# A two-block transformer on one core: the norm stages with column-group sums, small roots and joined phases

## The reference, cut to what matters

```python
def rmsnorm(x, g):
    xf = x.astype(jnp.float32)
    y = xf * lax.rsqrt(jnp.mean(xf * xf, axis=-1, keepdims=True) + RMS_EPS)
    return (y * g.astype(jnp.float32)).astype(x.dtype)
...
x = x + gt1 * rmsnorm_2(y, p['g_post_mix'])
h = modulate(rmsnorm_2(x, p['g_pre_ffn']), sh2, sc2)
x = x + gt2 * rmsnorm_2(conv_ffn(h, p), p['g_post_ffn'])
```

## Time and profile before

| what | us |
|---|---|
| median of 3 runs (lowest to highest) | 3000.8 (2995.47 to 3001.47) |
| the profiled execution | 3002.31 |
| its span, first to last instruction | 3000.5 |
| PE busy (of the span) | 2717.9 (91%) |
| DVE busy | 1418.4 (47%) |
| ACT busy | 516.1 (17%) |
| POOL busy | 162.8 (5%) |
| mean granted TensorE clock | 0.943 |

### The profile page before, as it was taken

One profiled execution on the slowest core, in us unless ns is written; L12 is line 12 of the kernel. 1 busy time (PEld: TensorE's weight loads), 2 busy tenths in 40 slices (PEclk: granted clock), 3 DMA queues, 4 the chain that ended last, 5 costly groups with the idle time before them and its releaser, 6 DMA issues.

```text
span 3000.5 us, 46544 instructions
## 1 busy us (share of the span) xinstructions
PE 2717.9 (91%) x20206; PEld 1974.1 (66%) x20206; DVE 1418.4 (47%) x2486; ACT 516.1 (17%) x1033; POOL 162.8 (5%) x112
## 2 busy tenths in 40 slices
PE   7989999998999898999999988997778769999996
PEld 3643788886645445888884743546777733788885
DVE  3153655525004436555424365254444463877624
ACT  2121100001013322000001032013333211122100
POOL 0000000000000000000000000003333200000000
PEclk9979999999998989999999977997999979999998
DMA  5313222233120002232234101200000013222231
GB/s 189 97 36 98 71 85 85 67 100 100 57 84 1 1 30 83 93 96 84 58 99 128 42 15 56 56 1 2 4 4 4 4 57 98 71 85 84 67 91 53
DMA packets 219563, 190.34 MB, mean 63 GB/s; under 512 B 8667, under 2 KB 216956, under 8 KB 219360
## 3 DMA queue, kind: packets, MB, share of 16 engines
q1 hardware_dynamic: 219066, 187.27, 20.2%
q10 hardware_dynamic: 294, 0.09, 0.0%
HBM read 185.25 MB, written 2.10 MB: 62 GB/s over the span
## 4 chain that ended last, share of the span: by engine, by line
PE 81%; DVE 12%; issue 2%; ACT 2%; DVEq 0%; DMA 0%; POOLq 0%; POOL 0%; ACTq 0%; SPq 0%
PE psum L1138 26%; PE psum L335 18%; PE psum L1348 13%; PE psum L365 4%; PE psum L2041 4%; PE psum L2048 3%; PE psum L778 2%; PE psum L800 2%; DVE sbuf L277 1%; PE psum L786 1%; PE psum L776 1%; DVE sbuf L290 1%; PE psum L2118 1%; PE psum L1751 1%; DVE sbuf L2431 1%
## 5 line engine op out<-in xcount | busy, mean ns | idle before, releaser
L1138 PE MATMUL psum<-sbuf 128*128 128x256 f32 x3696 | 810.6, 383 | 9.9 <-DVE sbuf L1197 6.5
L1138 PEld LDWEIGHTS psum<-sbuf 128*128 128x128 f32 x3696 | 708.7, 192 | 110.8 <-DVE sbuf L1197 7.7
L335 PE MATMUL psum<-sbuf 128*128 128x512 f32 (+5 forms) x1424 | 542.4, 543 | 22.7 <-DVEq L434 22.5
L335 PEld LDWEIGHTS psum<-sbuf 128*128 128x128 f32 (+3 forms) x1424 | 264.5, 187 | 295.8 <-issue 257.1
L1348 PE MATMUL psum<-sbuf 128*128 128x256 f32 x1848 | 405.2, 382 | 12.4 <-DVE sbuf L1365 6.8
L1348 PEld LDWEIGHTS psum<-sbuf 128*128 128x128 f32 x1848 | 353.8, 192 | 63.5 <-DVE sbuf L1365 7.6
L1222 DVE TENSOR_TENSOR sbuf<-sbuf,psum 128x256 f32<-128x256 f32 x462 | 177.7, 415 | 205.7 <-PE psum L1138 204.5
L2048 PE MATMUL psum<-sbuf 64*64 64x64 f32 x4992 | 204.8, 232 | 32.6 <-issue 19.1
L2041 PE MATMUL psum<-sbuf 64*64 64x64 f32 (+1 forms) x4544 | 180.0, 233 | 50.3 <-DVE sbuf L2409 30.6
L2048 PEld LDWEIGHTS psum<-sbuf 64*64 64x64 f32 x4992 | 180.0, 143 | 44.2 <-issue 38.1
L2041 PEld LDWEIGHTS psum<-sbuf 64*64 64x64 f32 x4544 | 164.5, 141 | 57.1 <-DVE sbuf L2409 32.0
(11 more groups left out here) (232 smaller groups left out, 2516.7 us busy)
## 6 DMA issues: line engine op xcount, KB each, us to landing
sbuf<-in_w_mod_dram SPq DMA_DIRECT2D x24, 1024.0 KB, 5.2
sbuf<-in_w_ffn_gate_dram SPq DMA_DIRECT2D x22, 1024.0 KB, 5.5
sbuf<-in_w_ffn_up_dram SPq DMA_DIRECT2D x22, 1024.0 KB, 7.3
sbuf<-in_w_ffn_down_dram SPq DMA_DIRECT2D x32, 704.0 KB, 6.2
...
```

The source lines that it names most:

```text
L335: mm = pe.matmul(bank, w[:, q, c0:c0 + m], rhs(k0 + q), start=start and q == 0, stop=stop and q == kc - 1)
L1138: mm = pe.matmul(bank, w[:, q, :], rhs[:, q, :], start=q == 0, stop=q == 3)
```

## The change

Each norm becomes three small steps. `column_sums` does not make one product of 512 tokens but four of 128, with 32 columns of `k.means` as weights and each with its output in its own 32 partitions of a PSUM bank: the means of the 512 tokens lie in 128 columns and four groups of partitions. ACT takes the root there with epsilon as bias, DVE the reciprocal in place, both over 128x128. `spread_columns` brings them back: four 128x128 products with one column of the identity, broadcast, as weights, into a PSUM bank of 128x512, from which DVE then scales.

In the post-norm the last two squares are no longer added on DVE but summed on PE, the product's phase and the norm phase are one (`joined`), and ACT loads the table with the root at the start of the product's phase (`load_root_table`). In the update POOL adds the chunks 0, 2, 3, 5 and 6 through three buffers in SBUF, DVE the chunks 1, 4 and 7 through one in PSUM. Shifts of the pre-norm go to ACT. The `w_mod` tiles are taken in pairs, with their rows in two groups of 32 partitions and their matmuls in turn; one pair stands before the second norm's first sum, one after its second, and the copy out (two of 2x512) stands on ACT between the squares of chunks 6 and 7. The squares and sums of `aside` in `ffn_up` go one by one behind the units 1 to 8 of the phase.

```diff
...
+def column_sums(k, pe, out, sq, start, stop):
+
+    for t in range(4):
+        r = slice(32 * t, 32 * t + 32)
+        mm = pe.matmul(out[r, :], k.means[:, 0:32], sq[:, t * P:(t + 1) * P], start=start, stop=stop)
+    return mm
+
+
+def spread_columns(k, pe, out, root):
+
+    for t in range(4):
+        mm = pe.matmul(out[:, t * P:(t + 1) * P], k.ident[:, 32 * t:32 * t + 1].broadcast_to([P, P]), root, start=True, stop=True)
+    return mm
...
+POOL_CHUNKS = (0, 2, 3, 5, 6)
+VECTOR_CHUNKS = (1, 4, 7)
+UPDATE_ORDER = (("scale", 0), ("scale", 1), ("scale", 2), ("add", 1), ("scale", 3), ("scale", 4), ("scale", 5), ("add", 4),
+                ("scale", 6), ("scale", 7), ("add", 7))
+TMP_BANK, POST_BANK, PRE_BANK, SUM_BANK = 0, 1, 6, 7
...
+def post_sum_tensor(k, pe, j):
+    pe.wait_ge(j.added, (KD - 3) * (j.nth + 1))
+    column_sums(k, pe, j.sums, j.acc, True, False)
+    for n in (KD - 2, KD - 1):
+        pe.wait_ge(j.squared, KD * j.nth + n + 1)
+        mm = column_sums(k, pe, j.sums, j.sq[:, (n - 1) % 2, :], False, n == KD - 1)
+    mm.then_inc(j.summed, 1)
+
+
+def root_scalar(k, act, j):
+    act.wait_ge(j.summed, j.nth + 1)
+    act.activation(j.root, j.sums, ACT.Sqrt, bias=k.eps).then_inc(j.rooted, 1)
+
+
+def invert_vector(k, dve, j):
+    dve.wait_ge(j.rooted, j.nth + 1)
+    dve.reciprocal(j.root, j.root).then_inc(j.inverted, 1)
...
-def norm_phase(k, name, jobs, post=None):
...
+def norm_phase(k, name, pre, post=None, fills=None):
...
+        if post:
+            spread_tensor(k, pe, post)
+            if not pre:
+                return
+            fill(0)
+            pre_sum_tensor(k, pe, pre, range(0, 2))
+            fill(1)
+            pre_sum_tensor(k, pe, pre, range(2, KD))
+            fill(2)
+            spread_tensor(k, pe, pre)
+        else:
+            pre_sum_tensor(k, pe, pre, range(KD))
+            fill(0)
+            fill(1)
+            spread_tensor(k, pe, pre)
+            fill(2)
...
+        for c in range(KD):
+            pre_square_scalar(k, act, pre, c)
+            if post and fills and fills.scalar and c == KD - 2:
+                fills.scalar(k, act)
...
+                for q in range(KD):
+                    for i in range(2):
+                        mm = pe.matmul(out[own[i], 256 * n:256 * n + 256], self.SIL[:, q, :], w[i][:, q, :],
+                                       start=q == 0, stop=q == KD - 1)
+                        if q == KD - 1:
+                            mm.then_inc(k.half_done, 2)
...
-    post = make_norm(k, "ffn_post2", Y, S, [], A_SCR)
-    ph.append(ffn_down(k, "ffn_down2", 2, k.a["w_down_2"][0], post, "ffn_up2"))
-    ph.append(norm_phase(k, "layer_norm2", [], post=(post, lambda c: derived_col(k, "pf", c))))
+    post = PostNorm(k, Y, lambda c: derived_col(k, "pf", c), A_SCR)
+    stage = ffn_down(k, "ffn_down2", 2, k.a["w_down_2"][0], post, "ffn_up2")
+    ph.append(joined(stage, norm_phase(k, "layer_norm2", None, post)))
```

More of the change, by code:

```diff
@@ new lines, in spread_tensor, with update_vector @@
+def spread_tensor(k, pe, j):
+    pe.wait_ge(j.inverted, j.nth + 1)
+    spread_columns(k, pe, j.rstd, j.root).then_inc(j.spread, 1)
+def update_vector(k, dve, j):
+    own = k.bank[TMP_BANK]
+    dve.wait_ge(j.spread, j.nth + 1)
+    for what, c in UPDATE_ORDER:
+        if what == "scale":
+            if c in POOL_CHUNKS:
+                n = POOL_CHUNKS.index(c)
+                if n >= 3:
+                    dve.wait_ge(j.moved, len(POOL_CHUNKS) * j.nth + n - 2)
+                out = j.tmp[:, n % 3, :]
+            else:
+                n = VECTOR_CHUNKS.index(c)
+                if n >= 1:
+                    dve.wait_ge(j.renewed, 2 * (len(VECTOR_CHUNKS) * j.nth + n))
+                out = own
+            ins = dve.scalar_tensor_tensor(out=out, in0=j.src[:, c, :], scalar=j.gain(c), in1=j.rstd, op0=ALU.mult, op1=ALU.mult)
+            if c in POOL_CHUNKS:
+                ins.then_inc(j.scaled, 1)
+            else:
+                ins.then_inc(j.renewed, 1)
+        else:
+            n = 2 * (len(VECTOR_CHUNKS) * j.nth + VECTOR_CHUNKS.index(c))
+            dve.wait_ge(j.renewed, n + 1)
+            dve.tensor_tensor(k.H[:, c, :], k.H[:, c, :], own, ALU.add).then_inc(j.renewed, 1)
@@ new lines, in update_pool, with wait_updated, __init__ @@
+def update_pool(k, pool, j):
+    for n, c in enumerate(POOL_CHUNKS):
+        pool.wait_ge(j.scaled, len(POOL_CHUNKS) * j.nth + n + 1)
+        pool.tensor_tensor(k.H[:, c, :], k.H[:, c, :], j.tmp[:, n % 3, :], ALU.add).then_inc(j.moved, 1)
+def wait_updated(eng, j, c):
+    if c in POOL_CHUNKS:
+        eng.wait_ge(j.moved, len(POOL_CHUNKS) * j.nth + POOL_CHUNKS.index(c) + 1)
+    else:
+        eng.wait_ge(j.renewed, 2 * (len(VECTOR_CHUNKS) * j.nth + VECTOR_CHUNKS.index(c)) + 2)
+class PreNorm:
+    def __init__(self, k, src, outs, scratch, post=None):
+        self.src, self.outs, self.post = src, outs, post
+        self.sq, self.root = view(k.M, scratch, 2, S), view(k.M, scratch + 2 * S, P)
+        self.sums, self.rstd = k.bank[SUM_BANK][:, P:2 * P], k.bank[PRE_BANK]
+        self.before, k.outs = k.outs, k.outs + KD * len(outs)
+        self.nth, k.pres = k.pres, k.pres + 1
+        self.shifted, k.shifts = k.shifts, k.shifts + (KD if outs[0][2] is not None else 0)
+        self.normed = k.norm_sems["normed"]
+        s = k.pre_sems
+        self.squared, self.consumed, self.summed, self.rooted, self.inverted, self.spread, self.scaled = (s[x] for x in PRE_SIGNALS)
@@ new lines, in scale_vector, with shift_scalar @@
+def scale_vector(k, dve, j):
+    dve.wait_ge(j.spread, j.nth + 1)
+    for gain, dst, shift in j.outs:
+        for c in range(KD):
+            ins = dve.scalar_tensor_tensor(out=dst[:, c, :], in0=j.src[:, c, :], scalar=gain(c), in1=j.rstd,
+                                           op0=ALU.mult, op1=ALU.mult)
+            ins.then_inc(j.normed if shift is None else j.scaled, 1)
+def shift_scalar(k, act, j):
+    for gain, dst, shift in j.outs:
+        if shift is None:
+            continue
+        for c in range(KD):
+            act.wait_ge(j.scaled, j.shifted + c + 1)
+            act.activation(dst[:, c, :], dst[:, c, :], ACT.Identity, bias=shift(c)).then_inc(j.normed, 1)
@@ L511, in scalar @@
     def scalar(k, act):
+        if fills and fills.first_scalar:
+            fills.first_scalar(k, act)
         if post:
[L513 to L516 removed]
+            root_scalar(k, act, post)
+        else:
+            load_root_table(k, act)
+        if not pre:
+            return
+        for c in range(KD):
+            pre_square_scalar(k, act, pre, c)
+            if post and fills and fills.scalar and c == KD - 2:
+                fills.scalar(k, act)
@@ L543, in square_vector @@
[L543 to L558 removed]
+            update_pool(k, pool, post)
@@ L1557, in part @@
         k.plan += 4
-        sync0, vector0, scalar0 = phase.sync, phase.vector, phase.scalar
-        steps = phase.tensor if isinstance(phase.tensor, list) else [phase.tensor]
-        assert len(split) == len(steps)
-        out = k.psum[0:2, 512 * 5:512 * 7]
-        turned = k.bank[5][:, 0:16].rearrange("p (n two) -> p n two", two=2)
+        out = k.bank[5]
+        turned = [k.bank[4 - i][:, 0:8].rearrange("p (n two) -> p n two", two=2) for i in range(2)]
+        own = [slice(32 * i, 32 * i + 2) for i in range(2)]
         def sync(k, sp):
```

351 lines of the change are left out of this document (184 added, 167 removed).

## The result

The changed kernel takes 2927.0 us (median of four runs, 2922.97 to 2930.61) against 3001.1 for the kernel before (2995.47 to 3002.55): ratio 0.9756, 95% interval 0.9738 to 0.9775. The forecast was 2928, in a range of 2915 to 2966. The profiled execution took 2930.61.

What follows compares the result with a forecast made beforehand. PE was busy 91% of the span, with gains where the chain leaves it in norm stages. Terms summed to 73.5 us off 3002.3, giving 2928.8, or 2928 as median; range 2915 to 2945, to 2966 with rivals 2 and 3.

Steps and rivals of the forecast that it cites:

- A: First root of five norm stages: last square to first post-norm scale 4.4 us instead of 8.87 or 7.6; 19.9 saved.
- B: Update and second root, four w_mod stages: first post-norm to first pre-norm scale 14.25 us instead of 19.1; 19.4 saved.
- rival 3: Clock falls to 1.2 GHz at the spreads: D lost, each of four stages gives back about 3; 2945, chance 12%.
- C: Start of the next product: 3.8 us twice (ffn_norm0, ffn_norm1), 3.4 after ffn_norm2, 2.1 after layer_norm1; 13.1 saved.
- D: Clock in ffn_up0 and ffn_up1: without the gap no half-speed stretch behind it; 2.5 us twice, 5.0 saved.
- E: layer_norm0, bound by PE: first pre-norm scale at 740.9 instead of 743.54; 2.6 us saved.
- F: input_norm, bound by PE: pairs from about 31.3 to 40.1, lead at 42.5 instead of 50.16; 7.7 us saved.
- Rivals 1 and 2: 1: column groups take turns, 2982, chance 8%. 2: DVE and POOL still exclude each other, 2939 to 2950, 9%.
- 4 and 5: Rival 4: narrow passes neither overlap nor hold clock, about 3070, 3%. Rival 5: unseen wait holds stages, about 3000, 2%.

Runs made afterwards that it cites:

- late_copies: six_squares with the copies of the w_mod rows behind ACT's second root and their turning behind PE's second spread; 2904.6 us, ratio 0.9684.
- aside_ahead: The changed kernel with the squares and adds of aside back ahead of the first weight sums of ffn_up0 and ffn_up1; 2928.8 us, ratio 0.9762.
- split_pair: late_copies with the second half of the second w_mod pair moved behind the last column sum; 2894.2 us, ratio 0.9666.
- after_again: The changed kernel, unaltered, measured and profiled once more; 2930.2 us, ratio 0.9761.
- serial_tiles: The changed kernel with the w_mod tiles of a pair multiplied one after the other, not in turns; 2939.5 us, ratio 0.9809.
- own_sbuf: The changed kernel with DVE's own product of the update (chunks 1, 4 and 7) in SBUF instead of PSUM; 2930.0 us, ratio 0.9766.
- split_both: split_pair with the second half of layer_norm0's values products also moved behind the last column sum; 2908.6 us, ratio 0.9699.
- six_squares: The changed kernel with six square buffers instead of two in the pre-norm; 2913.8 us, ratio 0.9719.

## Why the prediction held, and where it did not

**A was right in mechanism and 0.6 too long each.** 4.4 was forecast, 3.78 came. The old root of `layer_norm1` was 8.31 and not the 7.6 that I had taken for it, which adds 0.7. The last column sum is 0.43 with its tail where I had 0.7, since the tails of narrow passes overlap, and the spread with its change of weights 1.16 where I had 1.5; the 0.3 in it for changing to full weights had no row behind it, and 1.16 is the 0.86 of the columns and 0.3. The root was 0.37 for 0.27; the row I took was a copy. The three ways of undoing it price its parts: width 2.2, drain 0.25, table 0.8. That is 3.2 of the 5.1 saved in `ffn_norm0`; the rest, the add and the epsilon that left DVE's part of the chain (0.69 each) with their handovers, was not tested by itself.

**B failed, by 8 of 19.** Only the update (7.3 for 7.7) was as forecast. Two steps failed.

The first is the sentence that PE is done at about 9, before ACT. PE's amount of work was right, its order was not looked at: the second pair stands ahead of six sums, and with two square buffers ACT cannot go on without those sums. I had added up each engine's work where the two are coupled chunk by chunk. Where the clock is full, in `layer_norm1` and `ffn_norm2`, this puts the end of the last square at 11.37 instead of 10.25: 1.1 in each of four stages, 4.5.

The second is the clock, which the sum put at nothing in these stages and left to rival 3. These two rows of the changed kernel are the first pair of `layer_norm1` and the second spread of `ffn_norm0`, 30 and 8 passes; the same 30 took 5.09 in `ffn_norm0`, the same 8 take 1.16 in late_copies.

```profile
1546.56 3.40 PE L1760 MATMUL psum<-sbuf 128*2 128x256 f32 x30
```

```profile
283.46 2.08 PE L306 MATMUL psum<-sbuf 128*128 128x128 f32 x8 [1.05 <-DVE sbuf L370]
```

The slow first pair moves the last square to 13.05 and 12.83 in `ffn_norm0` and `ffn_norm1`, 3.1 together; the slow spread costs 0.9 four times; with 0.3 more in the tail that is 7.1. Against these stands that the tail was forecast too long: 4.0, where it is 3.15 with a spread at full clock (`layer_norm0` of aside_ahead, `ffn_norm2` of late_copies). 4.07 came, near the forecast by luck, because half the clock made up for it. 4.5 + 7.1 - 3.4 = 8.2, the 8 that were missing.

So the order is the smaller part of the miss and the clock the larger. They are not independent: with six buffers and later copies, which touch only order and buffers, the second spread is at full clock in all four stages. The distance is then 11.6 to 13.1, below the 14.25 forecast, which had the copies in the chain. Why the first pair is slow in two stages and not in the two others no run shows.

**C and D were right**, at 12.6 for 12.6 in two stages and 11.3 by the way back; the wait of PE went as forecast, and aside_ahead brought both it and the half clock behind it back. After `layer_norm1` the same term failed (-0.6 for 2.1). There the lead, 16 passes at 0.43, ran partly at half clock behind the second root, as these rows of the changed kernel and of split_pair show (in late_copies it takes 7.11):

```profile
1563.75 9.67 PE L507 MATMUL psum<-sbuf 128*128 128x512 f32 x16 [1.69 <-ACT sbuf L464]
```

```profile
1537.55 7.10 PE L508 MATMUL psum<-sbuf 128*128 128x512 f32 x16 [1.03 <-ACT sbuf L465]
```

So rival 3 was in large part true: it had put about 3 at each of the four stages, and 1.8 on average came, with 2.6 more in the lead after `layer_norm1`. The stretch of half clock in `ffn_up0` did not only vanish, another one came behind the second root, where PE had stood idle before and after its narrow sums; 12% was too little for it. Two stretches of the changed kernel, columns as in the earlier trace rows:

```profile
287.00:290.00 3.00, 3.00 (x8) 2.35 (x7) 3.00 (x5) 0.00 (x0) 0.00 (x0) 0.50 0.10 34
...
293.00:296.00 3.00, 3.00 (x16) 2.64 (x15) 2.97 (x5) 1.67 (x2) 0.00 (x0) 1.00 0.00 0
```

The first products of `ffn_up0` in late_copies, and in split_pair with half a pair in the gap of the root:

```profile
273.00:276.00 3.00, 2.92 (x7) 2.40 (x8) 3.00 (x5) 0.00 (x0) 0.00 (x0) 0.50 1.10 349
```

```profile
272.00:275.00 3.00, 2.89 (x11) 1.80 (x12) 3.00 (x5) 0.00 (x0) 0.00 (x0) 1.00 1.08 354
```

From the first pre-norm scale to `ffn_down0` this is worth 1.2 (269.15 for 270.35); in `ffn_norm1` the same distance is 269.1 in both.

**E and F** had the right bound. `input_norm` gave 1.6 more in this profile: its pairs took 8.26 from 30.54 on, where I had them from 31.3 to 40.1. In after_again they began at 31.25 and the lead at 42.45, which is the 7.7 forecast, so the 1.6 is the scatter between executions. `layer_norm0` gave 1.0 less. The second spread at half clock is 0.9 of it, and the first 32 passes of the products took 8.76 where the next 32 took 7.17; its four last squares stood behind the values products besides, again for want of buffers. How these divide the rest was not tested.

**Rivals 1 and 2** fall by serial_tiles and own_sbuf, 4 and 5 by the time.

**The total** was right by 1 us, and that was luck: with its terms as they were read, this execution would have taken 3002.3 - 66.3 = 2936.0, and it took 2930.6. The rest is 4.4 from stretches that the change does not touch, and 1.0 unassigned.

## What to carry to other kernels

Where two engines hand small buffers to each other, a sum of each one's work is not a forecast: write down their order item by item, and ask of every block that is slipped in between whose buffers it holds. Independent matmul work belongs into the gap that a root or a reciprocal leaves, not ahead of the sums that feed it; there it cost at most 0.2 us and won up to 1.3. Read each distance together with the granted clock, since a forecast can meet the number with a term too long and a clock too low. And test small changes by the distance between two instructions in a stage, with a second profile of the same kernel beside it, not by the total.

## What the runs showed of the chip

Executions of one kernel differ by where the granted clock falls. In the twelve profiles of the changed kernel and its variants the recurrent loop, the same instructions in each, took 332.4 to 341.3 us. The six runs of split_pair lie in two groups, 2884.7 to 2896.6 (four) and 2907.3 and 2911.7, those of split_both at 2894.9 and at 2905.3 to 2913.5 (five). Part of it can be seen in `fox_attention`: the same first heads ran at 0.50 in six_squares and at 1.00 in late_copies (columns as in the earlier trace rows).

```profile
881.00:885.00 4.00, 4.00 (x12) 2.65 (x11) 0.94 (x4) 1.08 (x4) 0.00 (x0) 0.50 0.01 2
```

```profile
878.00:882.00 4.00, 4.00 (x16) 2.25 (x16) 2.03 (x8) 1.91 (x6) 0.00 (x0) 1.00 0.00 0
```

Between these two kernels that makes 6 us there and another 6 by the end of that phase. Which of the two comes up was not controlled by any edit here, and there is no profile of split_both from its upper group, so that its 2908.6 comes from this is likely and not shown. It is also why the order of split_pair and split_both stays open, and why the step from the changed kernel to split_pair is given as a range: 26 us by the stages (18.2 in the four with `w_mod`, 3.5 in `layer_norm0`, 2.6 in the lead after `layer_norm1`, 1.7 in `input_norm`, whose lead comes at 39.09 for 40.83), 33 by the medians.
